# A hybrid diffusion layer on one core: x in nine pieces and one adaLN block ahead, u tiles moved, a semaphore for each accumulating DMA

## The reference

```python
sh1, sc1, g1, sh2, sc2, g2 = ada_mod(c[:, None, :], ada_w[l], ada_b[l])   # silu(c) @ ada_w + ada_b
hn_lat = rmsnorm(h, norm1_g[l]) * (1.0 + sc1) + sh1
hn_ctx = rmsnorm(hc, norm1_g[l]) * (1.0 + sc1c) + sh1c                    # context tokens
mix_ctx, mix_lat = token_mixers(hn_ctx, hn_lat, w_in[l], ..., w_out[l], rope, not last)
h = h + g1 * mix_lat
h = h + g2 * conv_ffn(rmsnorm(h, norm2_g[l]) * (1.0 + sc2) + sh2, ffn_w_up[l], ...)
return rmsnorm(h, final_norm_g)

def conv_ffn(hn, w_up, conv_w, conv_b, w_down):
    u = dwconv(hn @ w_up, conv_w, conv_b)
    gate, val = jnp.split(u, 2, axis=-1)
    return (jax.nn.silu(gate) * val) @ w_down
```

## Time and profile before

| what | value |
|---|---|
| median of 3 runs | 2588.55 us (2587.79 to 2592.18) |
| the profiled execution | 2589.64 us, its span 2588.0 us |
| TensorE busy | 2504.0 us (97%) |
| TensorE weight loads busy | 2056.3 us (79%) |
| VectorE, ScalarE, GpSimd busy | 1551.2, 972.5, 257.9 us |
| mean granted clock of TensorE | 0.992 |
| moved by DMA | 464.34 MB, mean 179 GB/s |

### The profile page before, as it was taken

One profiled execution on the slowest core, in us unless ns is written; L12 is line 12 of the kernel. 1 busy time (PEld: TensorE's weight loads), 2 busy tenths in 40 slices (PEclk: granted clock), 3 DMA queues, 4 the chain that ended last, 5 costly groups with the idle time before them and its releaser, 6 DMA issues.

```text
span 2588.0 us, 34753 instructions
## 1 busy us (share of the span) xinstructions
PE 2504.0 (97%) x12808; PEld 2056.3 (79%) x12808; DVE 1551.2 (60%) x1832; ACT 972.5 (38%) x1254; POOL 257.9 (10%) x327
## 2 busy tenths in 40 slices
PE   4999999999999898999999999999999999999997
PEld 2788888888756576888888888888888878888886
DVE  5545544474274236336788888888888853333345
ACT  3222222222334324224355555655555532222222
POOL 1000000000106223000001001001000010000000
PEclk8999999999999999999999999999999999999999
DMA  9855565786405455432566666666666562323223
GB/s 358 326 227 202 212 219 197 263 313 230 150 14 140 123 122 169 173 122 82 169 184 197 193 209 200 198 200 206 197 195 215 165 240 101 134 100 134 100 89 110
DMA packets 126357, 464.34 MB, mean 179 GB/s; under 512 B 19432, under 2 KB 39832, under 8 KB 95560
## 3 DMA queue, kind: packets, MB, share of 16 engines
q1 hardware_dynamic: 85088, 315.76, 34.5%
q0 software_dynamic: 27200, 130.23, 18.2%
q10 hardware_dynamic: 14000, 17.44, 1.9%
HBM read 425.14 MB, written 37.45 MB: 179 GB/s over the span
## 4 chain that ended last, share of the span: by engine, by line
PE 55%; DVE 2%; issue 1%; DMA 1%; ACT 1%; POOL 0%; SPq 0%; DVEq 0%; ACTq 0%; POOLq 0%
PE f_ps L2778 25%; PE f_late_ps L2834 8%; PE f_ps L2834 7%; PE f_late_ps L2837 4%; PE f_first_ps L2834 4%; PE f_ps L2837 3%; PE f_first_ps L2837 2%; DMA f_s<-in_w_up 1%; DVE h L2744 0%; PE f_late_ps L2802 0%; DVE f_lo L2421 0%; PE f_ps L2789 0%; DVE x_both L2600 0%; DVE f_u_lo L2459 0%; DVE h L2594 0%
## 5 line engine op out<-in xcount | busy, mean ns | idle before, releaser
L2206 ACT ACTIVATE f_hi<-f_raw 128x1024 fp32r<-128x1024 f32 x200 | 211.8, 1060 | 195.4 <-PE f_late_ps L2837 72.9
L2493 DVE TENSOR_TENSOR f_lo<-f_raw,f_hi 128x1024 fp32r<-128x1024 f32 x200 | 244.6, 1223 | 33.1 <-ACT f_hi L2206 33.0
L2778 PE MATMUL f_ps<-f_u_hi,f_hi 128*128 128x512 f32 x671 | 262.6, 391 | 1.5 <-DVE f_lo L2421 1.5
L2778 PE MATMUL f_ps<-f_u_hi,f_lo 128*128 128x512 f32 x671 | 262.6, 391 | 0.0
L2778 PE MATMUL f_ps<-f_u_lo,f_hi 128*128 128x512 f32 x671 | 262.5, 391 | 0.0
L2526 DVE SCALAR_TENSOR_TENSOR h<-f_ps,mod,h 128x512 f32<-128x512 f32 (+1 forms) x76 | 57.1, 751 | 318.0 <-PE f_ps L2778 318.0
L653 PE MATMUL i_ps<-hn,i_hi 128*128 128x512 f32 x608 | 237.5, 391 | 0.0
L2174 ACT ACTIVATE f_hi<-f_raw 128x1408 fp32r<-128x1408 f32 (+1 forms) x82 | 123.2, 1503 | 294.7 <-PE f_ps L2778 276.3
L2778 PE MATMUL f_ps<-x_both,f_hi 128*128 128x512 f32 x608 | 188.5, 391 | 1.8 <-PEq L1202 1.8
L647 PE MATMUL i_ps<-hn,i_hi 128*128 128x512 f32 x608 | 187.8, 390 | 0.0
L2421 DVE TENSOR_TENSOR f_lo<-f_raw,f_hi 128x1408 fp32r<-128x1408 f32 (+1 forms) x82 | 145.9, 1779 | 57.2 <-ACT f_hi L2174 56.8
(11 more groups left out here) (390 smaller groups left out, 5042.1 us busy)
## 6 DMA issues: line engine op xcount, KB each, us to landing
f_raw<-in_w_up SPq DMA_DIRECT2D x88, 1024.0 KB, 5.1
i_ring<-in_ada_rest POOLq DMA_DIRECT2D x64, 1024.0 KB, 5.3
f_raw<-in_w_down SPq DMA_DIRECT2D x64, 704.0 KB, 4.0
i_raw<-in_w_in SPq DMA_DIRECT2D x38, 1024.0 KB, 4.9
i_ring<-in_ada_first SPq DMA_DIRECT2D x32, 1024.0 KB, 7.3
f_s<-in_w_up SPq DMA_DIRECT2D x40, 512.0 KB, 7.6
f_raw<-in_w_up POOLq DMA_DIRECT2D x40, 512.0 KB, 5.5
f_s<-in_w_up POOLq DMA_DIRECT2D x40, 512.0 KB, 6.9
```

The lines of the kernel that those rows point to most:

```text
L2206: nc.scalar.activation(slot_of(w_hi, q), source(par, q), ACT.Copy).then_inc(bh_ok, 1)
L2493: nc.vector.tensor_tensor(slot_of(w_lo, q), source(par, q), slot_of(w_hi, q).bitcast(F32), ALU.subtract).then_inc(bl_ok, 1)
L2778: mm = nc.tensor.matmul(pt[s][:, :], m[:, k, :], v(k, slice(0, SEQ)), start=(k == 0 and n == 0), stop=(k == len(ks) - 1 and n == 2))
```

## The change

- x and the context are loaded in nine pieces, seven of two tiles and two of one (`PIECES` is (0, 2, 4, 6, 8, 10, 12, 14, 15, 16)), each with a semaphore; ScalarE's squares wait for the piece of their tile.
- `rstd` and the sum of squares move from `i_raw` to a place under the low halves of `w_in`'s weights, and the first `w_in` load no longer waits for the front's columns.
- `normed` is gone: one operation multiplies x by scale and `rstd`, in two spans (512 latent, 256 context columns); ScalarE adds the shift as it makes the high half, VectorE as it makes the low half. For column 0 the latent span is finished ahead of the context reciprocal.
- `first_products` of column j - 1 (instead of j - 2) follows `ada_block` j. Column 0's latent products start after block 1. In a step one output tile of five, not three, stands ahead of `ada_column`.
- The second accumulating DMA of each pair gets the semaphore `sb_ok`, for all pairs, and waits for the former pair's one. `block_high` q 1 and `block_sum` q 2 wait for the first DMA alone.
- Even groups' u tiles, and tiles 8 to 10 of odd groups, go where the token forms in `x_hi`, `x_lo` and `x_raw` lie, each as two rows of 256 columns; odd groups' first eight go to 97920 on. h of the down-products goes to 15872 (`h_low`). Down-products read their operand and write PSUM as two pieces of 256 columns. For group 0 tiles 0 to 3 are fetched after part 0 of the last pair (part 1 before), tiles 4 to 7 after part 3 (part 2 before), the first quarter of h after part 2 (part 4 before).
- In the last pair ScalarE splits all eleven u tiles ahead of `block_middle`, VectorE tiles 4 to 10 between the first `fold` and the first `block_outer`.
- The semaphore `neg_ok` is merged into `sd_ok`.

The diff, cut to its core:

```diff
@@ front: loads of x @@
-                for n in range(4):
-                    at = slice(4 * n, 4 * n + 4)
+                for n in range(len(PIECES) - 1):
+                    at = slice(PIECES[n], PIECES[n + 1])
@@ front: SyncE, after the adaLN blocks @@
-                sp.wait_ge(xn, KT)
                 load(sp, 0, 0)
@@ front: ScalarE @@
-                    act.wait_ge(fl, 2 * (j + 1))
-                    nc.scalar.activation(hn_hi[:, j, :], x32(j), ACT.Copy).then_inc(hh, 1)
+                def hn_high(j, n):
+                    act.wait_ge(fl, 2 * j + n + 1)
+                    a, b = SPANS[n]
+                    nc.scalar.activation(hn_hi[:, j, a:b], x32(j, a, b), ACT.Identity, bias=mod[:, j, n:n + 1]).then_inc(hh, 1)
+                row_copy(0)
+                first_w_hi(0)
+                hn_high(0, 0)
+                row_copy(1)
+                hn_high(0, 1)
+                first_w_hi(1)
...
@@ front: VectorE @@
                 dve.wait_ge(rt, 1)
                 nc.vector.reciprocal(rstd[:, 0:SEQ], rstd[:, 0:SEQ]).then_inc(rs, 1)
-                dve.wait_ge(rt, 2)
-                nc.vector.reciprocal(rstd[:, SEQ:TOK], rstd[:, SEQ:TOK]).then_inc(rs, 1)
-                dve.wait_ge(rs, 2)
-                normed(0)
...
-                    for n, (a, b) in enumerate(((0, SEQ), (SEQ, TOK))):
-                        nc.vector.tensor_scalar(x32(j, a, b), x32(j, a, b), scl[:, j, n:n + 1], mod[:, j, n:n + 1], ...)
...
-                    if j + 1 < KT:
-                        normed(j + 1)
-                    nc.vector.tensor_tensor(hn_lo[:, j, :], x32(j), hn_hi[:, j, :].bitcast(F32), ALU.subtract)
+                    scaled(j, 0)          # x * scl * rstd, 512 latent columns, one scalar_tensor_tensor
+                    if j == 0:
+                        first_w_lo(0)
+                        hn_low(0, 0)
+                        dve.wait_ge(rt, 2)
+                        nc.vector.reciprocal(rstd[:, SEQ:TOK], rstd[:, SEQ:TOK]).then_inc(rs, 1)
+                        dve.wait_ge(rs, 2)
+                        scaled(0, 1)
+                        hn_low(0, 1)      # (x + mod) - hi, one scalar_tensor_tensor
+                        continue
+                    scaled(j, 1)
+                    first_w_lo(j)
+                    for n in range(2):
+                        hn_low(j, n)
@@ front: TensorE @@
-                for j in range(KT):
+                ada_block(pe, 0)
+                ada_column(pe, 0)
+                ada_block(pe, 1)
+                first_products(pe, 0, slice(0, 1), (0,))
+                ada_column(pe, 1)
+                first_products(pe, 0, slice(1, NF), (0,))
+                first_products(pe, 0, slice(0, NFB), (1,), done=True)
+                for j in range(2, KT):
                     ada_block(pe, j)
-                    if j >= 2:
-                        first_products(pe, j - 2, slice(0, 3))
+                    first_products(pe, j - 1, slice(0, 1))
                     ada_column(pe, j)
-                    if j >= 2:
-                        first_products(pe, j - 2, slice(3, NF))
-                first_products(pe, KT - 2, slice(0, NF))
-                first_products(pe, KT - 1, slice(0, NF))
+                    first_products(pe, j - 1, slice(1, NF), done=True)
+                first_products(pe, KT - 1, slice(0, NF), done=True)
@@ tail: places of the u tiles and of h @@
-        u_at = [[15872 + 4096 * j for j in range(8)] + [159360 + 4096 * j for j in range(3)],
-                [142976 + 4096 * j for j in range(4)] + [175744 + 4096 * j for j in range(7)]]
+        h_low = ground.at("h_down", [P, KT, SEQ], 15872)
+        def u_tile(name, tiles, b, j):
+            if b == 0 or j >= 8:
+                k = (2 * j if b == 0 else 2 * (j - 8)) if j < 8 or b == 1 else HK + 2 * (j - 8)
+                at = slice(0, SEQ // 2) if b == 0 and j < 8 else slice(SEQ // 2, SEQ)
+                return tiles[:, k:k + 2, at]      # tiles: x_hi, x_lo, x_raw
+            skip, kind = (0, F32R) if name == "hi" else (2048, F32R if name == "lo" else F32)
+            return ground.at(f"f_u_{name}{b}_{j}", [P, 2, SEQ // 2], 97920 + 4096 * j + skip, kind)[:, :, :]
@@ tail: GpSimd @@
                                    accum_op=ALU.add).then_inc(sa[par], 16)
                     pool.wait_ge(sx[par], 16 * (r + 1))
+                    if positive(i):
+                        pool.wait_ge(sb_ok, 16 * i)
                     pool.dma_start(S_buf[par][:, :, :], ..., accum_op=ALU.add)
-                                   .then_inc(sa[par], 16)
+                                   .then_inc(sb_ok, 16)
...
-                pool.wait_ge(pq_ok, 7 * last + 2)
+                pool.wait_ge(pq_ok, 7 * last + 1)
                 get_u(0, 0, 4, u_first[0])
-                pool.wait_ge(pq_ok, 7 * last + 3)
+                pool.wait_ge(pq_ok, 7 * last + 4)
                 get_u(0, 4, 8, u_first[1])
@@ tail: SyncE @@
-                sp.wait_ge(bl_ok, 7 * PAIRS)
-                sp.wait_ge(pq_ok, 7 * last + 5)
-                sp.dma_start(h[:, 0:4, :], hd[:, 0:4, :]).then_inc(h_ld[0], 16)
+                sp.wait_ge(pq_ok, 7 * last + 3)
+                sp.dma_start(h_low[:, 0:4, :], hd[:, 0:4, :]).then_inc(h_ld[0], 16)
@@ tail: ScalarE, block_high and the last pair @@
-                elif q in (1, 4):
-                    act.wait_ge(sa[par], 32 * (r + 1))
+                elif q == 1:
+                    act.wait_ge(sa[par], 16 * (r + 1))
+                elif q == 4:
+                    act.wait_ge(sb_ok, 16 * (i + 1))
...
-                        for j in range(8):
+                        for j in range(GT):
                             u_high(act, 0, j)
                     block_middle(act, i, 0)
...
-                        for j in range(8, GT):
-                            u_high(act, 0, j)
@@ tail: VectorE, block_sum q 2 and the last pair @@
-                    dve.wait_ge(sa[par], 32 * (r + 1))
+                    dve.wait_ge(sa[par], 16 * (r + 1))
...
-                        for j in range(4, 8):
-                            u_low(dve, 0, j)
                     part_add(dve, i, 5, par)
                     fold(dve, i, 0)
                     if not last:
                         block_low(dve, i + 1, 1, 1 - par)
+                    else:
+                        for j in range(4, GT):
+                            u_low(dve, 0, j)
                     block_outer(dve, i, 0)
...
-                        for j in range(8, GT):
-                            u_low(dve, 0, j)
@@ tail: TensorE, product(..., pieces=True) for all down-products but the last two @@
+                to = pt[s][:, :].rearrange("p (a t) -> p a t", a=2) if pieces else pt[s][:, :]
```

More of the change, by code:

```diff
@@ L661, in product, with first_products @@
                 mm.then_inc(mm_ok, 1)
-            def first_products(pe, k, part):
-                pe.wait_ge(hl, k + 1)
+            def first_products(pe, k, part, spans=(0, 1), done=False):
+                pe.wait_ge(hl, 2 * k + spans[-1] + 1)
                 pe.wait_ge(wfl, k + 1)
@@ L2763, in _, with product @@
                     scaled(n)
-            def product(pe, t, s, ks, v_hi, v_lo, first=False, free=None, tiles=None, loaded=None):
+            def product(pe, t, s, ks, v_hi, v_lo, first=False, free=None, tiles=None, loaded=None, pieces=False):
                 pe.wait_ge(lo_ok, t + 1)
@@ L2891, in _, with hidden @@
                     t = D0 + KT * g
+                    def hidden(tile, at):
+                        return tile if at == slice(0, SEQ) else tile[:, 0 if at == EARLY else 1, :]
                     def hidden_hi(k, at):
-                        return u_hi[g % 2][k][:, at]
+                        return hidden(u_hi[g % 2][k], at)
                     def hidden_lo(k, at):
-                        return u_lo[g % 2][k][:, at]
+                        return hidden(u_lo[g % 2][k], at)
                     if g == 0:
                         product(pe, t, 0, ks, hidden_hi, hidden_lo, free=(ev_ok, D0), tiles=(down_hi, down_lo),
-                                loaded={k: (ul_ok, k + 1) for k in ks})
-                        product(pe, t + 1, 1, ks, hidden_hi, hidden_lo, free=(ev_ok, D0))
+                                loaded={k: (ul_ok, k + 1) for k in ks}, pieces=True)
+                        product(pe, t + 1, 1, ks, hidden_hi, hidden_lo, free=(ev_ok, D0), pieces=True)
                     else:
```

146 lines of the change are left out of this document (77 added, 69 removed).

## The result

The changed kernel took 2574.04 us in the median of four runs (2572.02 to 2574.95), the kernel before 2590.36 us (2587.79 to 2592.39). The ratio is 0.994, with a 95% interval from 0.9928 to 0.9953: faster by about 15.5 us. 2573.5 was forecast. The profiled execution took 2574.95 us with a span of 2573.3, 14.7 less than the 2588.0 of before.

The account below looks back on a forecast made before the run. TensorE was busy 2504 of 2588 us, so only its idle time, slow matmuls and order of work could pay. -8.7 - 5.5 - 5.3 + 4.3 = -15.2 us took the median of 2588.55 to 2573.5, range 2568 to 2581.

Parts of the forecast that it names:

- Front: Start of the kernel: smaller x pieces, a shorter VectorE chain and earlier first products bring the first `w_in` product to 153.7, -8.7 us.
- bound of 40.5: Front: latest predicted end of adaLN block 1, where `first_products` of column 0 starts, with the x gain gone; 39.2 was expected.
- bound of 37.6: Front: earliest predicted start of column 0's `first_products`, with block 1 taking the 1.93 us of a later block at 2.4 GHz.
- rival of 4 us: Front gives only about 4 us because small x pieces come later or the blocks are late: 2578 us, chance 0.12.
- The semaphores: Opening of the pair products: waiting only for the first accumulating DMA removes 3.9 us of waiting and 1.6 of slow clock, -5.5.
- The u tiles: Down-products of even groups: moving low-lying u tiles higher brings 7.65 us a product to 7.48, -5.3 us over 32 products.
- the form: Down-products reading their operand and writing PSUM in two pieces of 256 columns: 0 taken; rival that it costs, 2603, chance 0.03.
- The rule of a read port of its own for the weights: Skill's rule by which a u tile's place should not matter; rival that place doesn't matter: 2578.8 us, chance 0.15.
- The end of the pairs: Last pair: u tiles split first delay down-product 1, TensorE waits 4.2 instead of 1.5 us; +4.3 with slow clock.
- The clock's term: End of the pair products: slow matmuls after the wait for down-product 1, +1.6 us, taken from the opening's 3.75 us wait.
- five terms: Front -8.7, semaphores -5.5, u tiles -5.3, end of the pair products +2.7 waiting and +1.6 slow clock; sum -15.2 us.

## Why the prediction was right

**Front.** Right in its chain, by its own marks: the ones-product at 28.23 (27.9), the end of its way on VectorE at 38.2 (37.9), block 1's end and the first products at 39.28 (39.2), the first `w_in` product at 153.1 (153.7). One thing in it was told wrongly. I reckoned with the arrival of pieces; once the pieces are small, VectorE's ten additions in a row set the end of the sum of squares, and ScalarE's last waits are for VectorE. Two more things. The bound of 40.5 "with the x gain gone" was added wrongly, 39.2 + 2.2 is 41.4, and four pieces gave 41.63; the bound of 37.6 left out VectorE's own 37.9. And the size was in part luck: block 1 took 3.37 us in this profile, near the 3.6 of the sum, but 1.93 in four other profiles of the same front, so the front's gain lies anywhere from 8.2 to 10.4 us. The rival of 4 us, because small pieces load worse, is out: 333 against 334 GB/s, and nine pieces are worth 2.4 us. The Trainium skill, "DMA: Bandwidth & Descriptors", section "Bandwidth", asks for transfers of 1 MiB or more; the nine pieces (512 and 256 KB, before 1024 and 512) break that, and nothing of it is seen here, where several are in flight at once.

**The semaphores.** Right in place and cause. The size was 6.2 instead of 5.5: the trace of before had a further wait of 0.45 us in front of pair 0's part at 1306.28, which the sum left out.

**The u tiles.** The size was right (7.65 to 7.48 in 32 products), and that the form costs nothing was right. The reason is narrower than what I wrote: not how low a tile lies, but how many bytes past a multiple of 512 it starts. The change gained because all its new places start 128 past one in the arena. The rule of a read port of its own for the weights ("TensorE: Matmul & The Clock Gate", section "Step-by-step: what each phase is for", in the Trainium skill) is not contradicted by that; it says nothing about a start, and a rule on the weights alone was no ground to expect that places are alike.

**The end of the pairs.** The step was right, with 2.9 instead of 2.7 us of waiting. The clock's term was mis-sized: 1.6 was taken from the opening, and it was 2.8. The runs show that it isn't a fixed price. After waits of 4.0 to 4.6 us for down-product 1, its add followed that of 0 after 9.53, 9.56, 9.59, 10.73, 10.77 and 10.81 us, against 7.95 and 7.99 where the wait was 2.31 us or filled: 1.6 to 2.8 us. Waits of 5.1 to 5.7 us, in four other kernels, cost no more (9.72 to 10.33), so the price doesn't follow the wait's length either.

**What held the sum together.** The five terms missed by -0.6, +0.3, -0.7, +1.4 and +0.1: the total of 0.5 is partly luck, the single terms are within 1.4 us. The clock of TensorE, in the front and at the end of the pairs, moves a profile by more than that 0.5: 1.1 us less in the front and 1.2 less at the end of the pairs were measured in other profiles.

## What to carry to other kernels

List the starts of the operands that stream through TensorE, not only which memory they share: here 128 bytes more or less decided over 2% of a product's time, and a run that shifts one buffer tells. Take the distances as measured here with care: know from where your addresses count, and try more than one shift. When a stage's end is reordered, write down for each engine what stands behind the instruction that waits for a transfer: three small copies ahead of the gate cost 5 us inside the trace here, and the two kernels that put them back behind it have the lowest medians. Two DMAs on one semaphore make every reader wait for the later one; here it cost only where the pipeline starts, so look there first.

## What the runs showed of the hardware that I had not expected

- Matmuls of 512 float32 columns go by 7.0 to 7.6 ns slower each when the moving tile starts 0, 64 or 256 bytes past a multiple of 512 in the arena than when it starts 128 past one (7.65, 7.66, 7.64 against 7.48 us a product), at 15872 on as well as at 97920 on. With the arena at byte 18496 of the memory the slow starts are 64, 128 and 320 past a multiple of 512, the fast one 192. In all of these the weights start where the fast tiles do, at 128 past one in the arena.
- A wait of 4.0 to 4.6 us at the same place costs a different stretch of slow clock from kernel to kernel, though nothing nearby was edited (1.6 to 2.8 us, and not always more for the longer wait: 2.8 behind 4.19 us, 1.6 behind 4.31); the granted clock stood at 0.51 for the six microseconds behind 4.60 us of idle time, and at 1.00 behind 2.31 us.
- With TensorE busy from 21.4 to 28.7 us before them, the first ones-products took 1.13 us instead of 2.04, and still block 1 at 35.2, behind 1.76 us of idle time and other gaps, ran at a clock of 0.57 in one profile and at 1.00 in another (3.58 and 1.93 us). Without that filling it does the same: 1.93 us in four profiles, 2.68 to 3.61 in five.
